# Attention outputs with the probabilities as TensorE's weights: rows first, scaled once per kind of head, then turned

## What is computed

```python
z = x @ w_in
fq, fk, fv, ff, sq, sk, sv = jnp.split(z, IN_SPLITS, axis=-1)
# fox: 8 heads of 64, causal, decay bias c[t] - c[s], 128-query blocks
s = einsum('bqhd,bkhd->bhqk', qi, k) * scale + ci[..., :, None] - c[:, :, None, :]
p = softmax(where(kpos <= qpos, s, -inf))
y_fox = einsum('bhqk,bkhd->bqhd', p, v)
# swa: 8 heads, 2 shared K/V heads, window of 2 chunks of 64, ALiBi bias, a sink per head
p = softmax(concatenate([s, sink]))[..., :band]
y_swa = einsum('bckgqr,bcrkd->bcqkgd', p, vb)
mix = concatenate([y_fox, y_swa]) @ w_out
x = layer_norm(alpha * x + mix)
x = layer_norm(alpha * x + peer_layer(x))
```

## Time and profile before

| | |
|---|---|
| median of 3 runs | 1451.15 us (1450.85 to 1452.06) |
| the profiled execution | 1450.84 us |
| its span | 1449.2 us |
| time around the span | 1.64 us |
| PE busy | 1425.9 us, 98% of the span |
| DVE, ACT, POOL busy | 1043.7, 608.0, 1016.1 us |
| the four pairs | about 48 to 203 us of the span |
| granted clock of PE | 0.997 over the span |

### The profile page before, as it was taken

How to read it: one execution, slowest core, us unless ns; L and a number is a source line. 1 busy time by engine, 2 the same in 40 slices (tenths; PEclk the granted TensorE clock), 3 DMA queues, 4 the chain that set the end, 5 groups by cost and what they waited for, 6 DMA issues and landing times.

```text
span 1449.2 us, 24866 instructions
## 1 busy us (share of the span) xinstructions
PE 1425.9 (98%) x8029; PEld 1267.5 (87%) x8029; DVE 1043.7 (72%) x2204; ACT 608.0 (42%) x1018; POOL 1016.1 (70%) x631
## 2 busy tenths in 40 slices
PE   9999999999999999999999999999999999999996
PEld 5888778889999999999999999888888888888885
DVE  5466666688999999899986694865555555555597
ACT  5666741334333354444444443433333333333332
POOL 3332331335598878888887689988888888888886
PEclk9999999999999999999999999999999999999998
DMA  6212120424599989999999899999999999999981
GB/s 240 74 59 102 59 88 4 149 81 126 171 348 330 294 271 376 375 409 414 396 365 384 311 399 396 348 395 365 347 367 359 353 344 350 352 354 351 361 306 58
DMA packets 136907, 406.96 MB, mean 281 GB/s; under 512 B 13904, under 2 KB 56656, under 8 KB 134672
## 3 DMA queue, kind: packets, MB, share of 16 engines
q1 hardware_dynamic: 97088, 263.48, 50.8%
q0 software_dynamic: 39760, 142.76, 25.0%
HBM read 355.50 MB, written 50.14 MB: 280 GB/s over the span
## 4 chain that ended last, share of the span: by engine, by line
PE 85%; DVE 6%; DMA 3%; issue 2%; ACT 2%; POOL 1%; SPq 0%; DVEq 0%; ACTq 0%; POOLq 0%
PE banks L1827 14%; PE banks L1829 13%; PE banks L1828 13%; PE banks L1882 12%; PE banks L1884 12%; PE banks L1883 12%; PE banks L1944 2%; POOL lo L456 1%; PE banks L2100 1%; PE banks L2101 1%; DVE rows L1366 1%; PE banks L2037 1%; DMA gelu_scratch<-gelu 1%; PE banks L1928 1%; DMA raw<-u_t 1%
## 5 line engine op out<-in xcount | busy, mean ns | idle before, releaser
L456 POOL TENSOR_TENSOR lo<-raw,hi 128x1024 fp32r<-128x1024 f32 x291 | 703.3, 2418 | 344.5 <-ACT hi L450 329.6
L1827 PE MATMUL banks<-x1T_hi,hi 128*128 128x368 f32 (+3 forms) x1168 | 395.3, 338 | 0.5 <-POOL lo L456 0.3
L1828 PE MATMUL banks<-x1T_lo,hi 128*128 128x368 f32 (+3 forms) x1168 | 390.0, 334 | 0.0
L1829 PE MATMUL banks<-x1T_hi,lo 128*128 128x368 f32 (+3 forms) x1168 | 389.9, 334 | 0.0
L450 ACT ACTIVATE hi<-raw 128x1024 fp32r<-128x1024 f32 x291 | 305.8, 1051 | 31.9 <-DMA raw<-u_t 19.1
L1882 PE MATMUL banks<-hi,wgt_hi 128*128 128x512 f32 x750 | 291.9, 389 | 0.3 <-DVE wgt_lo L1704 0.3
L1883 PE MATMUL banks<-lo,wgt_hi 128*128 128x512 f32 x750 | 291.8, 389 | 0.0
L1884 PE MATMUL banks<-hi,wgt_lo 128*128 128x512 f32 x750 | 291.8, 389 | 0.0
L1704 DVE TENSOR_TENSOR wgt_lo<-wgt,wgt_hi 128x384 fp32r<-128x384 f32 x125 | 91.9, 736 | 193.1 <-ACT wgt_hi L1119 192.9
L1827 PEld LDWEIGHTS banks<-x1T_hi,hi 128*128 128x128 f32 x1168 | 219.3, 188 | 5.0 <-DVE x1T_lo L1338 0.6
L1829 PEld LDWEIGHTS banks<-x1T_hi,lo 128*128 128x128 f32 x1168 | 219.2, 188 | 4.4
(11 more groups left out here) (239 smaller groups left out, 1757.7 us busy)
## 6 DMA issues: line engine op xcount, KB each, us to landing
raw<-u_t SPq DMA_DIRECT2D x128, 512.0 KB, 5.6
raw<-v_tab SPq DMA_DIRECT2D x128, 512.0 KB, 5.7
g_scratch<-stage SPq DMA_DIRECT2D x12, 2048.0 KB, 10.8
gelu_scratch<-gelu SPq DMA_DIRECT2D x116, 192.0 KB, 7.3
ga<-gelu_scratch SPq DMA_DIRECT2D x29, 768.0 KB, 7.5
gg<-g_scratch SPq DMA_DIRECT2D x14, 1536.0 KB, 11.2
raw<-w SPq DMA_DIRECT2D x26, 512.0 KB, 3.3
raw<-w_pq SPq DMA_DIRECT2D x16, 512.0 KB, 3.4
```

The source lines that it names most:

```text
L456: eng.tensor_tensor(l[:, :], raw[:, c % RAW_SLOTS, :], h[:, :].bitcast(F32), ALU.subtract).then_inc(lo_ready, 1)
L1827: pe.matmul(o, h[:, s], hiT[:, k, tokens], start=(k == 0), stop=False)
L1828: pe.matmul(o, h[:, s], loT[:, k, tokens], start=False, stop=False)
L1829: ins = pe.matmul(o, l[:, s], hiT[:, k, tokens], start=False, stop=(k == KT - 1))
```

## The change

Six things are changed; all of them are in the stage of the pairs and right behind it.

1. In `mix` the turned probabilities of a block of keys are the weights and one head's 64 columns of values move. The output has the queries on its partitions, and 64 columns for each head of each block of queries; each head sums on its own. `vv` and `swa_v` lose their zero-padded halves (and DVE its two clears; ACT copies the values in one instruction).
2. Probabilities are no longer scaled. `turn` waits for the exponentials, and `normalise` only puts the reciprocals of the sums in the new tile `norms`.
3. A new DVE step `take_mixed` multiplies the whole bank 6 + g, 128x512, by the reciprocals and writes `mixed_rows`. It stands at step 3 for the swa outputs of the pair before and at step 11 for the fox outputs of this one.
4. A new PE step `turn_mixed` transposes `mixed_rows` in four pieces back into the same bank. It stands behind the logits of steps 4 and 12, and once behind the last pair.
5. `outputs_hi` waits for these transposes. For the swa outputs it stays at step 4; for the fox outputs it moves from step 11 to 12, and `outputs_lo` from 12 to 13.
6. Behind the last pair, PE does three `mix_block` calls of the second block of frames ahead of the last one of the first, around the last `turn_mixed`.

```diff
-        swa_v = sb("swa_v", [P, TB, 2, P], F32, att)
-        vv = sb("vv", [P, TB, 2, P], F32, att)
+        swa_v = sb("swa_v", [P, TB, P], F32, att)
+        vv = sb("vv", [P, TB, P], F32, att)
+        mixed_rows = [sb(f"mixed_rows{g}", [P, SEQ], F32, att) for g in range(2)]
...
-        OUTPUT_AT = 4
+        OUTPUT_AT = MIX_LAG + 1
...
             def outputs_hi(j, g):
-                act.wait_ge(head_mixed, NU * j + SWA_UNITS * (g + 1))
+                act.wait_ge(mixed_turned, 2 * j + (g + 1))
...
-                    if step == SWA_UNITS + MIX_LAG:
+                    if step == SWA_UNITS + OUTPUT_AT:
                         outputs_hi(j, 0)
...
-            dve.memset(vv[:, :, :, :], 0.0)
-            dve.memset(swa_v[:, :, :, :], 0.0)
...
+            def take_mixed(j, g):
+                dve.wait_ge(head_mixed, NU * j + SWA_UNITS * (g + 1))
+                dve.wait_ge(norm_step, (NU + SWA_UNITS) * j + SWA_UNITS * (2 * g + 1))
+                dve.tensor_tensor(mixed_rows[g][:, :].rearrange("p (b d) -> p b d", b=2 * TB),
+                                  banks[:, 6 + g, :].rearrange("p (b d) -> p b d", b=2 * TB),
+                                  norms[:, g, :, :].rearrange("p b a -> p (b a)").unsqueeze(2).to_broadcast([P, 2 * TB, HD]),
+                                  ALU.mult).then_inc(mixed_taken, 1)
...
-                    dve.tensor_scalar(probs[u % 4][:, 0:nk * P], probs[u % 4][:, 0:nk * P], r[:, 4:5], 0.0,
-                                      ALU.mult, ALU.add, accum_out=r[:, 6:7]).then_inc(probs_ready, 1)
...
+            def turn_mixed(j, g):
+                pe.wait_ge(mixed_taken, 2 * j + (g + 1))
+                for b in range(TB):
+                    ins = pe.transpose(banks[:, 6 + g, bass.ts(b, P)], mixed_rows[g][:, bass.ts(b, P)], ident[:, :])
+                ins.then_inc(mixed_turned, 1)
...
-                    pe.wait_ge(probs_ready, NU * j + (u + 1))
+                    pe.wait_ge(exp_ready, NU * j + (u + 1))
...
-                    o = banks[:, 6 + (kind == "swa"), bass.ts(qb, P)]
+                    o = banks[:, 6 + (kind == "swa"), bass.ts(2 * qb + a, HD)]
...
-                        ins = pe.matmul(o, val[:, k0 + k, a, :], probs_t[u % 2][:, k, :], start=(a == 0 and k == 0),
-                                        stop=(a == 1 and k == nk - 1))
+                        ins = pe.matmul(o, probs_t[u % 2][:, k, :], val[:, k0 + k, own(a)], start=(k == 0), stop=(k == nk - 1))
...
+            mix_block(0, KT - 2)
+            mix_block(1, 0)
+            turn_mixed(PAIRS - 1, 1)
+            for i in range(1, BLOCK_AHEAD):
+                mix_block(1, i)
             for b in range(TB):
-                for i in range(KT - 2 if b == 0 else 0, KT):
+                for i in range((KT - 1, BLOCK_AHEAD, 0, 0)[b], KT):
```

More of the change, by code:

```diff
@@ L848, in copy_values @@
                 act.wait_ge(v_turned, n + 1)
-                for a in range(2):
-                    ins = act.activation(dst[:, :, a, own(a)],
-                                         banks[:, bank, :].rearrange("p (b d) -> p b d", b=TB)[:, :, own(a)], ACT.Copy)
-                ins.then_inc(proj_copied, 1)
+                act.activation(dst[:, :, :], banks[:, bank, :].rearrange("p (b d) -> p b d", b=TB),
+                               ACT.Copy).then_inc(proj_copied, 1)
             def split_heads(value, bank, dst, scale=1.0, twice=None):
@@ L1231, in normalise @@
                     dve.wait_ge(exp_ready, NU * j + (u + 1))
-                    steps = (NU + SWA_UNITS) * j + (u + count_swa(u))
+                    norm = norms[:, int(kind == "swa"), qb, a:a + 1]
                     if kind == "fox":
-                        dve.reciprocal(r[:, 4:5], r[:, 2:3]).then_inc(norm_step, 1)
-                        dve.wait_ge(norm_step, steps + 1)
+                        dve.reciprocal(norm, r[:, 2:3]).then_inc(norm_step, 1)
                     else:
                         dve.tensor_scalar(r[:, 5:6], r[:, 2:3], r[:, 3:4], None, ALU.add).then_inc(norm_step, 1)
-                        dve.wait_ge(norm_step, steps + 1)
-                        dve.reciprocal(r[:, 4:5], r[:, 5:6]).then_inc(norm_step, 1)
-                        dve.wait_ge(norm_step, steps + 2)
-                    dve.tensor_scalar(probs[u % 4][:, 0:nk * P], probs[u % 4][:, 0:nk * P], r[:, 4:5], 0.0,
-                                      ALU.mult, ALU.add, accum_out=r[:, 6:7]).then_inc(probs_ready, 1)
+                        dve.wait_ge(norm_step, (NU + SWA_UNITS) * j + (u + count_swa(u) + 1))
+                        dve.reciprocal(norm, r[:, 5:6]).then_inc(norm_step, 1)
                 for step in range(NU):
@@ L1250, in pair @@
                         projected_lo(3, j)
+                    if step == MIX_LAG and not first:
+                        take_mixed(j - 1, 1)
                     if step == OUTPUT_AT + 1 and not first:
                         outputs_lo(j - 1, 1)
-                    if step == SWA_UNITS + MIX_LAG + 1:
+                    if step == SWA_UNITS + MIX_LAG:
+                        take_mixed(j, 0)
+                    if step == SWA_UNITS + OUTPUT_AT + 1:
                         outputs_lo(j, 0)
@@ L1265, in _ @@
             pair(PAIRS - 1, last=True)
+            take_mixed(PAIRS - 1, 1)
             outputs_lo(PAIRS - 1, 1)
@@ L1949, in pair @@
                     logits(step)
+                    if step == OUTPUT_AT and not first:
+                        turn_mixed(j - 1, 1)
+                    if step == SWA_UNITS + OUTPUT_AT:
+                        turn_mixed(j, 0)
                     if last and step in FILL_AT:
```

5 lines of the change are left out of this document (4 added, 1 removed).

## The result

| | before | changed |
|---|---|---|
| median | 1450.84 us (21 runs) | 1453.05 us (21 runs, 1451.24 to 1457.16) |
| the profiled execution | 1450.84 us | 1451.24 us |
| its span | 1449.2 us | 1449.6 us |
| PE busy | 1425.9 us | 1427.8 us |
| DVE busy | 1043.7 us | 1011.2 us |

The ratio is 1.0016 with a 95% interval of 1.0008 to 1.0023: the changed kernel is slower by about 2.3 us (1.2 to 3.3). Predicted were +2.3 us and 1453.2 us, and the time lies in what the prediction called "same" (up to 1454.05 us). The size came out, but not by the steps of the sum: several savings were larger than I put them, or missing, and a cost that isn't in it made up for them.

The account below looks back on a forecast made before the run. PE was taken as the bound. Transposes and ACT's copy at 3.1 us, with -0.4, -0.25, -0.2 and +0.05, summed to +2.3 us, put down as 1453.2 us; range 1449.0 to 1457.0 us.

Parts of the forecast that it names:

- The passes: The 272 mixing passes on PE: the weight load sets their 0.112 us distance, so halving the moving columns gives 0.
- Transposes of step 4 in pairs 1 and 2: The added PE transposes there count in full, as no wait stands behind step 4: 2 x 0.45 us.
- Step 12 of pairs 0 to 2: outputs_hi ahead of the keys' copies makes ACT, and PE waiting for it, later: 3 x 0.59 in place of 3 x 0.45 us.
- The last pair's transposes: The added transposes in the last pair vanish in PE's waits for ACT at 180.53 and 196.41: 0 us.
- Rival 1: Nothing absorbs: the last pair's waits move on with PE, turning stays behind ACT; +3.9 us, 1454.9 us; chance 0.18.
- (a): Last pair: PE idles until DVE splits the swa queries; without the scaling directly ahead of that split, -0.4 us.
- (b): Behind the last pair, turning units 14 and 15 no longer waits for scalings; ACT takes part back: -0.25 us.
- (c): PE's wait for mix_lo at 204.77 goes, covered by three mix_block calls of the second block: -0.2 us.
- The last transposes: The one turn_mixed behind the last pair adds its four transposes to PE: 0.45 us.
- The layer norm: The first block's sum is ready three calls later; its norm just holds before turn_x1: +0.05 us, bounds 0 and 0.4.
- Rival 3: take_mixed's multiplication takes 1.28 us and misses PE at each step 12 and step 4; +5.1 us, 1456.2 us; chance 0.08.
- the cover of 0.2 us: At step 11 the multiplication would end at about 78.6, before PE wants the transposes at 78.82: 0.2 us to spare.

## Why the prediction was right, step by step

- **The passes: 0.** Right, and shown by three widths of the moving side and two of the weights.
- **Transposes of step 4 in pairs 1 and 2: 0.9.** Right: doubling them cost 0.47 and 0.52 us a pair, and 0.45 is left when the cost of step 12 is gone.
- **Step 12 of pairs 0 to 2: 3 x 0.59.** The mechanism is right; each is 0.48 us, 0.11 less than I put. The chain runs over ACT, and moving that one copy took the whole cost away, while doubling the transposes added none. But the term is the time until ACT's next instruction starts, not the copy's own length. In the changed kernel that is 80.57 - 80.09 on ACT:

```profile
80.09 0.59 ACT L902 ACTIVATE mix_hi<-banks 128x512 fp32r<-128x512 f32 x1
80.57 1.19 ACT L860 ACTIVATE k_both<-banks 64x512 fp32r<-64x512 f32 x2
```

- **The last pair's transposes: 0.** Right; the shift stays at 1.42 to 1.46 us across both, and the waits are gone. Rival 1 (they count in full) is out: even twice as many came through with only 0.4 us.
- **(a) The swa queries: -0.4.** Measured -0.39 (1.81 to 1.42). **(b) The turning behind the pairs: -0.25.** Measured -0.26: the first output matmul behind the last mixing stands at 204.31, 1.20 us later than before (203.11), and the shift had been 1.46.
- **(c) The wait for `mix_lo`: -0.2.** Gone, and worth 0.31: in the kernel before, the two distances around it are 205.11 - 204.34 = 0.77 us, where two without a wait are 0.46.

```profile
204.34 0.39 PE L1884 MATMUL banks<-w_hi,mix_lo 128*128 128x512 f32 x1
204.77 0.50 PE L1882 MATMUL banks<-w_hi,mix_hi 128*128 128x512 f32 x1
205.11 0.40 PE L1883 MATMUL banks<-w_lo,mix_hi 128*128 128x512 f32 x1
```

- **The last transposes: 0.45.** Measured 0.43: the starts around them are 206.96, 207.54 and 207.86, 0.90 us for two distances of 0.233.
- **Pair 0's first turning.** Missed: PE turns unit 0 without waiting for its scaling, and the shift goes from -0.33 to -0.57 us there. -0.24 us. I had written that the removal is worth nothing in the steps; in the very first ones there is no work a step ahead to cover it.
- **The layer norm: +0.05.** Measured 0. DVE ends at 217.29 + 1.28 = 218.57, so it is 0.25 us early, and PE starts `turn_x1` 0.23 us behind its last matmul:

```profile
218.59 0.40 PE L1894 MATMUL banks<-w_hi,mix_lo 128*128 128x512 f32 x1
218.82 1.03 PE L2018 MATMUL banks<-ident,x 128*128 128x128 f32 x8
```

- **The address of the weights: +0.8 to 1.0.** Not in the sum: nothing in the prediction's working asks what the new tile `norms` moves. It is no part of what the change means to do; it comes with the place in which a tile of 64 bytes was put.
- **Rival 3 (`take_mixed` late).** It didn't happen, at 0.684 us for one: at step 12 of pair 0 the multiplication ends at 77.92, and the transposes start at 78.27. It does happen as soon as the scalings are kept: the cover of 0.2 us that I called the thinnest is given by their removal.

So the measured terms give 0.9 + 3 x 0.48 + 0 + 0.43 - 0.24 - 0.39 - 0.26 - 0.31 + 0.95 = +2.5 us, which is what the mark shows, and my sum was 2.3. It lacked the address's +0.95 and pair 0's -0.24, step 12 was 0.33 too dear in all, (c) 0.11 too small and the layer norm 0.05 too dear, and these nearly cancelled. The result is right by about as much luck as method: without the 64 bytes it would have been about +1.5 us.

## What to carry to other kernels

Price an instruction that is put ahead of others by the distance from its start to the next one's, and look one step on for idle time that takes it for nothing: here one line moved by one step gave back 1.5 of 2.5 us. When a change adds a tile, check which weight tiles move with it. And before making TensorE's matmuls smaller, see what sets their distance, and what the clock does in stretches where PE also waits.

## What the runs showed of the hardware

- Weight tiles of fp32r that start 64 bytes past a multiple of 256 give matmuls of 512 columns a distance of 0.233 us in place of 0.227, in three pairs of kernels that differ in it (the kernel before with and without the unused tile, and the changed kernel with `norms` ahead or behind, once with `mix_hi` copied at step 12 and once at step 13). Other offsets weren't tried.
- An f32 matmul with 128 columns of weights has a distance of 0.112 us whether 16, 64 or 128 columns move. With 64 columns of weights it is 0.064 (the loads 0.057 apart), and each run of such loads among loads of 128 columns loses some 0.3 us.
- Less work can be slower by the clock. With 16 columns moving in place of 64, in steps where PE waits the same 1.0 us in 4, the granted clock fell to the level of 1.2 GHz for 6.8 and for 3.4 us; with PE waiting 1.2 us in 4 and 64 columns it fell for about 3.4 us. In the profiled executions of the kernel before (1.2 us in 4 there too, 128 columns) and of the changed kernel it stays at 1.00. No rule follows from these single executions, as some of the kernel before have a lower mean clock as well.
- On ACT the next instruction starts 0.48 us after a copy of 512 columns that is listed with 0.59 us.
